# Four modulation units beside the linear attention's output projection: from TensorE to VectorE

## The reference

```
mod_x = einsum('bd,lde->lbe', silu(c), w_ada) + b_ada[:, None, :]
mod_c = einsum('d,lde->le', silu(c_ctx), w_ada) + b_ada
...
x = x + g1 * ox                       # ox: the attention's output through w_o
x = x + g2 * swiglu(rmsnorm(x, norm_ffn[i]) * (1.0 + sc2) + sh2, ffn_w_in[i], ffn_w_out[i])
```

## Time and profile before

| | |
|---|---|
| runs | 1608.48, 1609.16, 1609.93 us; median 1609.16 |
| profiled execution | 1610.13 us, of which span 1608.4 us |
| busy in the span | TensorE 97%, VectorE 59%, ScalarE 42%, GpSimd 6% |
| granted TensorE clock, mean | 0.99 of full speed |

### The profile page before, as it was taken

The page is one execution under the profiler, slowest core; times in us unless marked ns, Lnnn a source line. Parts: engine busy times, 40 slices in busy tenths (PEclk is TensorE's granted clock), DMA queues, the critical chain, the costliest instruction groups (busy, mean ns, idle before and its releaser), DMA issues.

```text
span 1608.4 us, 22707 instructions
## 1 busy us (share of the span) xinstructions
PE 1562.1 (97%) x9052; PEld 1333.9 (83%) x9052; DVE 956.1 (59%) x1564; ACT 669.7 (42%) x1063; POOL 100.2 (6%) x95
## 2 busy tenths in 40 slices
PE   7999999999999999999999999989999999999997
PEld 5787788888878898989898998867778888888886
DVE  5665536544585655878787757888746433333324
ACT  5225457543363341523242445568734421221222
POOL 0000000000000000000000000056620000000003
PEclk9999999999999999999999999999999999999999
DMA  9342300013233544335333313420002332332332
GB/s 336 116 135 79 105 26 27 28 53 105 80 105 118 158 131 144 105 122 166 109 115 118 88 58 105 116 69 1 2 27 83 101 105 82 101 104 89 94 92 92
DMA packets 195790, 156.43 MB, mean 97 GB/s; under 512 B 7138, under 2 KB 190606, under 8 KB 195694
## 3 DMA queue, kind: packets, MB, share of 16 engines
q1 hardware_dynamic: 195694, 155.10, 31.7%
HBM read 149.84 MB, written 2.10 MB: 94 GB/s over the span
## 4 chain that ended last, share of the span: by engine, by line
PE 77%; DVE 10%; ACT 6%; DMA 3%; issue 2%; SPq 1%; DVEq 0%; ACTq 0%
PE ps L697 75%; DVE w_lo L2047 1%; PE ps L1293 1%; DMA w_raw<-in_ffn_w_in 1%; ACT w_hi L1411 1%; ACT pr L2001 1%; DVE scaled L2103 1%; DMA ada_pre<-in_w_ada 1%; DVE u_acc L2161 1%; DVE h_lo L2112 1%; DVE t_lo L2632 1%; DVE q_st L2852 1%; PE ps L1298 1%; ACT h_hi L1461 1%; DVE t_sum L2627 1%
## 5 line engine op out<-in xcount | busy, mean ns | idle before, releaser
L697 PE MATMUL ps<-h_hi,w_lo 128*128 128x512 f32 (+2 forms) x936 | 337.7, 361 | 0.0
L697 PE MATMUL ps<-h_hi,w_hi 128*128 128x512 f32 (+1 forms) x784 | 294.0, 375 | 4.0 <-DVE w_lo L2047 3.8
L697 PE MATMUL ps<-h_lo,w_hi 128*128 128x512 f32 (+1 forms) x784 | 286.7, 366 | 0.0
L2047 DVE TENSOR_TENSOR w_lo<-w_raw,w_hi 128x2048 fp32r<-128x2048 f32 (+1 forms) x57 | 128.5, 2254 | 199.6 <-ACT w_hi L1411 199.5
L697 PEld LDWEIGHTS ps<-h_hi,w_lo 128*128 128x128 f32 x936 | 177.1, 189 | 24.3
L1411 ACT ACTIVATE w_hi<-w_raw 128x2048 fp32r<-128x2048 f32 (+1 forms) x57 | 107.4, 1884 | 194.3 <-DMA w_raw<-in_ffn_w_in 96.9
L697 PE MATMUL ps<-a_hi,w_lo 128*128 128x512 f32 (+1 forms) x528 | 187.0, 354 | 0.0
L697 PEld LDWEIGHTS ps<-h_hi,w_hi 128*128 128x128 f32 x784 | 148.6, 190 | 34.1 <-issue 5.6
L697 PEld LDWEIGHTS ps<-h_lo,w_hi 128*128 128x128 f32 x784 | 148.8, 190 | 24.1
L685 POOL TENSOR_SCALAR pr<-pr,rden 128x384 f32<-128x384 f32 x64 | 82.5, 1296 | 811.8 <-DVE rden L2919 811.5
L697 PE MATMUL ps<-a_hi,out_hi_w 128*128 128x512 f32 (+1 forms) x352 | 121.7, 346 | 2.8 <-DVE a_lo L2608 1.5
(11 more groups left out here) (325 smaller groups left out, 2972.3 us busy)
## 6 DMA issues: line engine op xcount, KB each, us to landing
w_raw<-in_ffn_w_in SPq DMA_DIRECT2D x88, 512.0 KB, 5.0
ada_w<-in_w_ada SPq DMA_DIRECT2D x41, 1024.0 KB, 5.2
w_raw<-in_gla_w_in SPq DMA_DIRECT2D x24, 512.0 KB, 4.8
w_raw<-in_ffn_w_out SPq DMA_DIRECT2D x40, 256.0 KB, 3.0
w_raw<-in_ffn_w_out SPq DMA_DIRECT2D x16, 512.0 KB, 4.0
ada_pre<-in_w_ada SPq DMA_DIRECT2D x7, 1024.0 KB, 11.6
w_raw<-in_gla_w_o SPq DMA_DIRECT2D x8, 512.0 KB, 6.8
w_raw<-in_swa_w_o SPq DMA_DIRECT2D x8, 512.0 KB, 4.7
```

Of the source, the lines that this page charges most:

```text
L697: return pe.matmul(o, w, r, start=start, stop=stop, skip_group_check=skip)
L2047: dve.tensor_tensor(w_lo[s][:, 0:kc, :], raw_of(n)[:, 0:kc, :], hi_of(n)[:, 0:kc, :].bitcast(F32), ALU.subtract).then_inc(wlo_ok, 1)
```

## The change

Units 8 to 11 go over to the path of `unit_acc`, `unit_sum` and `store_sum`. They use the second of the two accumulators (`u_set`). VectorE's accumulation is written behind the split of the next slab's weights and ahead of the slab's residual. TensorE's sum is at step 2 of the next slab. ScalarE's `unit_row` is gone in this stretch. The order of loads on SP is the same, and `ada_done` is now raised by the last instruction of the accumulation.

```diff
     def sum_no(a):
-        return a if a < V0 else a - U1 + V0
+        return a if a < V0 else a - V0 if a < 12 else a - U1 + 8
     def acc_base(a):
-        return 15 * min(sum_no(a), V0) + 7 * max(sum_no(a) - V0, 0)
+        return 15 * min(sum_no(a), 8) + 7 * max(sum_no(a) - 8, 0)
     def u_set(a):
-        return int(a >= U1)
+        return int(a >= 8)
...
-                    if z == len(passes) - 1 and k == kc - 1 and sums is not None:
+                    if z == 0 and k == 2 and sums is not None:
                         unit_sum(sums, 2 * i)
...
-            pe.wait_ge(row_ok, a - V0 + 1 + i)
+            pe.wait_ge(row_ok, a - V0 + 1 - 4 * int(a >= 12))
...
-        def first_slab(n, e, segs, turn=None):
+        def first_slab(n, e, segs, units=0):
...
-                if k == 2 and turn is not None:
-                    unit_turn(turn)
+                if k == 2 and units:
+                    unit_sum(units - 1)
                 if k == 3:
-                    if turn is not None:
-                        pe.wait_ge(mod_ok, turn + 2)
+                    if units:
+                        pe.wait_ge(mod_ok, units + 1)
                     statistics(m, tiles)
...
-                 turns=unit_of(n) - 1 if n > GO0 else None)
-            unit(unit_of(n))
+                 sums=unit_of(n) - 1 if n > GO0 else None)
...
-        first_slab(F0, 0, BOTH, turn=11)
+        first_slab(F0, 0, BOTH, units=12)
...
                 squares("gla", 2 * (n - GO0) + ch, 0)
-            unit_row(unit_of(n))
...
             split(n + 1)
+            unit_acc(unit_of(n))
             plain(n, "gla", 2 * (n - GO0), 16, BOTH, False)
             raw_low(0, 2 * (n - GO0), BOTH)
-            store_unit(unit_of(n))
+            store_sum(unit_of(n))
```

## The result

The changed kernel takes 1616.72 us (median of six runs, 1615.33 to 1618.88) against 1609.68 us for six runs of the kernel before beside it. The ratio is 1.0046 with a 95% interval of 1.0034 to 1.0057, thus slower by about 7 us. The forecast was 1615.3 us in a range of 1608 to 1618. The profiled execution took 1618.88 us, the longest of the six, with a span of 1617.2 us; the span in the profile before is 1608.4 us.

What follows compares the result with a forecast made beforehand. TensorE was taken to bound the kernel around O0 to O3. Waits of 8.1 us, less 4.4 us saved, plus 2.4 us of clock gave +6.1 us: 1615.3 us from 1609.16, range 1608 to 1618.

Steps and rivals of the forecast that it cites:

- The pace and the gain: Over output-projection slabs O0 to O3 TensorE never rests; four units leaving it, less four sums over partitions, save 4.4 us.
- The loop: Accumulation, load of unit and weights, rounding, split, next accumulation: turns of 18.6, 19.4, 19.4 us against TensorE's 17.2 us.
- The landings: Time from a unit load's issue to ScalarE's start on the weights behind it, taken as 8.19, 8.92 and 8.92 us.
- 3.7 us predicted: Lateness of the statistics in the first FFN slab F0, after waits of 8.0 to 8.1 us eat the 4.4 us.
- the point from which the change was to stop being a loss: Mean time of 7.4 us from a unit load's issue to ScalarE's start on the weights behind it.
- the fourth rival: More is lost: F0's spread also at half clock, or landings of 9.3 us; +8 to +9 us, 1617.5 us; chance 0.10.
- The waits: TensorE waits at the sums in O1, O2, O3 and F0, then ahead of F0's statistics: 8.0 to 8.1 us.
- The clock: After F0's 3.8 us wait TensorE drops to half clock, costing 2.4 us; bounds no loss and 3.9 us.
- the second rival: Waits as forecast, but the clock stays up: +3.7 us, 1612.9 us; chance 0.12.
- Half clock after O3's wait costs nothing: Half clock after the waits in O2 and O3 costs nothing, as TensorE's next wait of 2.2 or 3.8 us absorbs it.
- The sum: Whole forecast: 8.1 us of waits, less 4.4 us saved, plus 2.4 us of clock, +6.1 us.
- the likeliest case: The forecast itself, chance 0.58, spanning 1612.4 us (landings of 8.2 us, clock half lost) to 1617.5 us.

Runs made afterwards that it cites:

- the three versions that have no wait: Changed kernel with weights issued ahead of the unit (0.9964), half the accumulation (0.9965), or accumulation ahead of the split and unit 8's moved into the attention (0.9967).
- The filled wait: Changed kernel with 26 unread matmuls in TensorE's wait ahead of F0's statistics: 1614.57 us, ratio 1.0038 to the kernel before.

## Why the prediction was right, and where it was not

**The pace and the gain.** TensorE set the pace before, and its saving of 4.4 us was sized rightly: T falls by 4.2 to 4.3 us in the three versions that have no wait.

**The loop.** Shown. It was opened at three different places, and each time all waits at the sums and at the statistics went: the queue's order, VectorE's order, the length of the accumulation. Moving the place where TensorE waits only moved the wait.

**The landings.** Mis-sized. The step took 8.19, 8.92 and 8.92 us from the two landings of the trace before; measured were 8.20, 9.82 and 10.43. That is 2.4 us more. The trace before has a third landing that the prediction did not read, that of O3's weights, issued behind the unit load at 387.40:

```profile
396.41 1.92 ACT L1411 ACTIVATE w_hi<-w_raw 128x2048 fp32r<-128x2048 f32 x1 [4.67 <-DMA w_raw<-in_gla_w_o]
```

It took 9.01 us, so reading it would have added 0.1 us only. Unit 8's accumulation ended some 0.2 us earlier than worked out, and the rest of a turn took some 10.3 us instead of 10.44 three times, so unit 11's accumulation ended at 429.8 instead of 427.9, 1.9 us late. This is the whole difference between 3.7 us predicted and 5.63 us measured for the statistics. The mean landing of 9.5 us lies on the far side of the point from which the change was to stop being a loss, 7.4 us. In part the fourth rival came true, whose landings were 9.3 us: the measured median lies between the forecast and that rival's 1617.5 us. Why the landings grew is open. The estimate of 6.8 us from the fit of the Trainium skill (DMA: Bandwidth & Descriptors, section on the anatomy of one DMA), which was measured on loads that GpSimd issues, does not carry over to this queue: all three landings took longer, 8.20 to 10.43 us.

**The waits.** Predicted 0.1, 1.3, 2.2, 0.6 and 3.8 us, measured 0, 1.12, 2.84, 0.46 and 3.61. Their sum, 8.1 against 8.03, agrees by luck: the longer landings would have made more of it, but TensorE came later to F0's sum and to the statistics, by what it lost at half clock after O3's wait, 15.94 - 14.41 = 1.53 us.

**The clock.** The fall behind the wait in F0 came, so the second rival, in which the clock stays up, is out. Its cost was sized too small, 3.27 us instead of 2.4: from the statistics to the spread 442.47 - 436.36 = 6.11 us against 3.45, so 2.66 us, and 0.61 us of the spread itself, which the forecast had left at full clock and only its upper bound had counted. The filled wait shows the same 3.2 us from the other side.

**Half clock after O3's wait costs nothing.** True in the changed kernel, where TensorE had slack of 0.46 and 3.61 us left behind it. It is no property of the stretch: with unit 11 back on TensorE the same fall cost 1.6 us. The prediction's reason (the next wait takes it) was the right one, and my expectation for that experiment forgot it.

**The sum.** +8.9 us in the profiled execution against +6.1: 1.9 us by the landings, 0.9 by the clock. The median of the runs shows +7.0; the profiled execution was the longest of its six, so a smaller surplus in the others is likely but not shown. One bound of the likeliest case was added up wrongly: landings of 8.2 us with half of the clock's loss give 3.7 - 1.5 + 1.2 = 3.4 us, thus 1612.6 us and not 1612.4.

## What to carry to other kernels

Before work is moved to an engine that has time, follow which queue the new work's end releases, and add up the loop through that queue: a load that waits for a slow consumer holds up every load behind it, and an engine that is idle 40% of the span, as VectorE was here, becomes a part of the loop that sets the pace. Then look for the cheapest place to open the loop. Here it was the order of two loads in one queue, or of two steps on one engine, and each turned a loss of 7 us into a gain of 5.

## What the runs showed that was not expected

Loads of 2 MiB, issued in the same order on the same queue, landed after 8.2 to 10.4 us within one execution. The slowest is the one that brings F0's weights. There the issue of the two weight loads took 3.18 us, and in the kernel before 1.68:

```profile
406.49 1.68 SPq L481 DMA_DIRECT2D w_raw<-in_ffn_w_in  x2
```

Those 1.50 us are as much as this landing grew, 10.43 against 8.92. But the landing of O3's weights grew too, 9.82 against 9.01, with an issue of 1.13 us in both kernels. So the issue alone is not the cause, and none was tested.

A wait of TensorE of 1.97 to 2.01 us ahead of the third FFN slab is there in all ten kernels, whether the statistics start at 425 or at 436 us. It is set by the chain from the spread through ScalarE and VectorE, and none of these edits touches it.

Matmuls whose result nobody reads paid in kernels that wait: 18 and 26 of them in a wait kept the granted clock at full level where it otherwise averaged 0.6, and gave 1.55 and 3.2 us of TensorE's time in the stretch behind them. The kernels without a wait were faster still.
